# The values of the last two samples in split fp32r matmuls, in a two-layer hybrid decoder step

## The reference

```python
def past_kv(i):
    kp = cache_k[i, page_table].reshape(db, past_len, MOBA_HEADS, HEAD_DIM)
    vp = cache_v[i, page_table].reshape(db, past_len, MOBA_HEADS, HEAD_DIM)
    return kp, vp
...
        logits = jnp.where(allowed, logits, NEG_INF)
        p = jax.nn.softmax(logits.reshape(bsz, h, qc, r * MOBA_BLOCK), axis=-1).reshape(logits.shape)
        return jnp.einsum('bhqrs,bhqrsd->bhqd', p, vg.astype(jnp.float32)).astype(q.dtype)
```

## Time and profile before

| | us |
|---|---|
| median of 3 runs | 1311.08 (1310.75 to 1311.32) |
| span of the profiled execution | 1312.0 |
| TensorE busy | 1158.5 (88%) |
| VectorE busy | 734.8 (56%) |
| ScalarE busy | 570.3 (43%) |
| GpSimd busy | 265.6 (20%) |
| bytes read from HBM | 176.12 MB, 139 GB/s over the span |

### The profile page before, as it was taken

How to read it: one execution, slowest core, us unless ns; L and a number is a source line. 1 busy time by engine, 2 the same in 40 slices (tenths; PEclk the granted TensorE clock), 3 DMA queues, 4 the chain that set the end, 5 groups by cost and what they waited for, 6 DMA issues and landing times.

```text
span 1312.0 us, 21126 instructions
## 1 busy us (share of the span) xinstructions
PE 1158.5 (88%) x7223; PEld 999.5 (76%) x7223; DVE 734.8 (56%) x1165; ACT 570.3 (43%) x959; POOL 265.6 (20%) x250
## 2 busy tenths in 40 slices
PE   6999699787788778888979999997999799999995
PEld 4999588454445444442969999997999699999994
DVE  4843624486767666661366666444565566666333
ACT  3347202344654555541274444334424454444334
POOL 8301015100444445420220000021201220000011
PEclk9989859789989999999989999999999999999997
DMA  7324000433766666645624534433434334543421
GB/s 235 135 89 154 20 1 1 136 137 126 228 194 208 205 216 202 195 156 162 199 65 146 174 128 141 163 121 128 128 130 157 107 128 130 177 140 130 147 83 41
DMA packets 119112, 182.48 MB, mean 139 GB/s; under 512 B 6128, under 2 KB 59471, under 8 KB 118990
## 3 DMA queue, kind: packets, MB, share of 16 engines
q1 hardware_dynamic: 116274, 173.30, 40.5%
q0 software_dynamic: 2784, 8.47, 2.3%
HBM read 176.12 MB, written 5.63 MB: 139 GB/s over the span
## 4 chain that ended last, share of the span: by engine, by line
PE 70%; DVE 12%; ACT 9%; issue 5%; DMA 2%; POOL 1%; SPq 1%; DVEq 0%; ACTq 0%; POOLq 0%
PE bank L1621 65%; DVE kTl L1081 3%; ACT prob L899 2%; ACT kTh L686 2%; PE bank L1905 2%; ACT hi L686 1%; ACT xres L966 1%; POOL xl L629 1%; DVE xres L1081 1%; DMA vring<-cache_v 1%; DVE pen L1407 1%; PE bank L1922 1%; DVE prob L1416 1%; DVE rk L1081 1%; ACT xh L686 1%
## 5 line engine op out<-in xcount | busy, mean ns | idle before, releaser
L1621 PE MATMUL bank<-xh,hi 128*128 128x320 f32 x1184 | 372.9, 315 | 32.4 <-POOL xl L629 26.4
L1621 PE MATMUL bank<-xl,hi 128*128 128x320 f32 x1184 | 370.5, 313 | 0.0
L1621 PE MATMUL bank<-xh,lo 128*128 128x320 f32 x1184 | 370.4, 313 | 0.0
L1074 DVE TENSOR_TENSOR lo<-raw,hi 128x2048 fp32r<-128x2048 f32 x102 | 241.3, 2367 | 196.7 <-ACT hi L686 196.7
L1621 PEld LDWEIGHTS bank<-xh,hi 128*128 128x128 f32 x1184 | 226.7, 192 | 35.2 <-issue 29.8
L686 ACT ACTIVATE hi<-raw 128x2048 fp32r (+1 forms) x102 | 194.7, 1909 | 107.6 <-PE bank L1621 102.5
L1621 PEld LDWEIGHTS bank<-xl,hi 128*128 128x128 f32 x1184 | 226.9, 192 | 0.1
L1621 PEld LDWEIGHTS bank<-xh,lo 128*128 128x128 f32 x1184 | 226.4, 191 | 0.0
L606 POOL TENSOR_TENSOR lo<-vring,hi 128x1024 fp32r<-128x1024 f32 x48 | 114.6, 2390 | 177.6 <-ACT hi L686 177.6
L1081 DVE TENSOR_TENSOR kTl<-bank,kTh 128x512 fp32r<-128x512 f32 x128 | 87.6, 685 | 91.1 <-ACT kTh L686 89.7
L1621 PE MATMUL bank<-hh,hi 128*128 128x320 f32 x416 | 129.5, 311 | 1.3 <-DVE hraw L1081 1.3
(11 more groups left out here) (373 smaller groups left out, 1585.0 us busy)
## 6 DMA issues: line engine op xcount, KB each, us to landing
raw<-w_up SPq DMA_DIRECT2D x44, 1024.0 KB
kring<-cache_k SPq DMA_DIRECT2D x128, 256.0 KB, 3.7
vring<-cache_v SPq DMA_DIRECT2D x128, 256.0 KB, 3.3
raw<-w_down SPq DMA_DIRECT2D x8, 2048.0 KB
raw<-w_in_mix SPq DMA_DIRECT2D x7, 2048.0 KB
raw<-w_in_sc SPq DMA_DIRECT2D x8, 1024.0 KB
raw<-w_down SPq DMA_DIRECT2D x4, 1536.0 KB
raw<-w_out_mix SPq DMA_DIRECT2D x2, 2048.0 KB
```

Of the source, the lines that this page charges most:

```text
L1074: dve.tensor_tensor(lo[:, p], weight(n)[:, :, 256 * p:256 * p + 256], hi[:, p], ALU.subtract)\
L1621: return pe.matmul(out, lhsT, rhs, start=start, stop=stop, **kw)
```

## The change

`WHOLE` becomes `NB`, so that `whole(c)` is false for all samples: samples 6 and 7 take the way of the other six on every engine (rounding of V on ScalarE, difference on GpSimd, difference of the probabilities on VectorE, two fp32r matmuls a page, release of a ring group by `v_lo`). `split_hi(S_OUT, 1)` moves behind ScalarE's wait for `attn_mm`, since the tile half that it writes is in use for the rounded V until then.

```diff
--- before.py
+++ after.py
@@ -335,7 +335,7 @@
         UNITS, VUNITS = 16, 8
 
         pTf = raw[:, PAST + 512:PAST + 512 + 32 * (NPG + 1)].rearrange("p (j r) -> p j r", r=32)
-        WHOLE = NB - 2
+        WHOLE = NB
 
         def whole(c):
             return isinstance(c, int) and c >= WHOLE
@@ -941,9 +941,9 @@
             attend(NB - 2, NB - 3, NB - 4, NB - 1)
             attend(NB - 1, NB - 2, NB - 3, None, 1)
             attend(None, NB - 1, NB - 2)
-            split_hi(S_OUT, 1)
             attend(None, None, NB - 1)
             PE.wait(act, "attn_mm")
+            split_hi(S_OUT, 1)
             AC.up(copy(xh[:, 4:8, SEQ:TOK], bank[6][:, 0:256].rearrange("p (h c) -> p h c", h=H)), "attn_endh")
```

## The result

The changed kernel takes 1333.9 us (median of 4 runs, 1331.4 to 1334.7) against 1311.2 for the kernel before in the same series: ratio 1.0167, 95% interval 1.0152 to 1.0182, so 20 to 24 us slower. A second series in turns, longer and with more runs of before (17), gave 1332.7 against 1312.1: 1.0151, interval 1.0129 to 1.0172, so 17 to 23 us. The forecast was 1327, with a range up to 1333. Runs of one and the same kernel spread by some 8 us over these series (before: 1308.3 to 1316.4), so for terms of 1 to 5 us I read stage lengths within single profiles, which repeat better: the changed kernel profiled twice gave 28.2 and 28.2 for the first of its two stages, 26.9 and 27.2 for the second.

What follows compares the result with a forecast made beforehand. Bound: a round trip over V's ring of two groups, 6.3 us of load plus holding time. Later attn_mm 11.1, exposed splits 3.9 and lower clock 1.0 sum to +16.0 us on the 1311.1 median: 1327, range 1320 to 1333.

Steps and rivals of the forecast that it cites:

- (g): TensorE's clock at the projection and attention's last matmuls: lower level costs 1.0 us, bounds 0 and 3.
- (d): Three round trips of one V ring half, 12.2 us each, 36.6 in sum against 31.5: another 5.1 us.
- (a): Way into sample 6's first groups: sample 7's last bias on VectorE starts at about 582.0, +1.1 us.
- (b): Sample 7's ranks and shifts on VectorE, stretched beside GpSimd's differences: +2.8 us, bounds 0 and 4.6; shifts done 588.6.
- (c): After shifts, exponentials, then unit 3's copy and difference: ring's second half released at 594.2 instead of 588.9, late by 5.3.
- (e): Tail after the last difference: one unit and two own-key halves on TensorE, ending 632.5 against 621.43.
- (f): Splits of S_OUT half 1 between attn_mm and the projection, no longer hidden: gap 4.8 us instead of 0.92, +3.9.
- No price in (b) and (g): Rival: small VectorE operations slip into gaps; only delay (a), round trips and splits remain: +12, 1323; chance 0.20.
- TensorE is the bound: Rival: halves arrive in time in the last stages, TensorE's saving is won: about 8.6 us faster, 1302.5; chance 0.02.
- The stages hide the differences: Rival: GpSimd runs ahead, loads alone limit, (f) and little else remain: +5, 1316; chance 0.05.
- More collisions: Rival: VectorE operations or the clock hold up GpSimd or TensorE, two more 2.3 us waits: +20 to +21, 1332; chance 0.10.
- the opening claim: Values of samples 6 and 7: bound is a V ring round trip, 6.3 us load plus a group's holding time.

Runs made afterwards that it cites:

- e12: Changed kernel without the lo half of V for samples 6 and 7 (no differences, one matmul a page, less exact outputs): -0.1 us over before.
- e8: Changed kernel with V groups 2 and 3 of samples 6 and 7 loaded into the free K ring: +15.8 us over before.
- e4: Changed kernel with split_lo(S_OUT, 0) moved from the tenth stage into idle VectorE time in the first: +16.4 us over before.
- e1: Kernel before with only split_hi(S_OUT, 1) moved behind the wait for attn_mm: +3.3 us over before.
- e5: Changed kernel with four extra unused matmuls behind each unit of values but the last of samples 6 and 7: +16.0 us over before.
- e11: Changed kernel with the rounding of unit 3 of sample 6 ahead of sample 7's exponentials on ScalarE: +18.8 us over before.
- e6: e4 plus sample 7's differences of V made by VectorE instead of GpSimd: +12.0 us over before.
- e7: Kernel before, unsplit fp32, with V groups 2 and 3 of samples 6 and 7 loaded into the free K ring: -7.0 us over before.
- e10: Changed kernel with xh and xl ahead of half 1's splits, split_lo(S_OUT, 0) early, and sample 7's differences on VectorE: +7.0 us over before.
- e3: Kernel before with only sample 6 going through the halves, sample 7 staying in unsplit fp32: +12.6 us over before.

## Why the prediction was wrong

Direction and mechanism were right; the size was 16.0 us against 19.8 by stages. The first median, 1333.9, lies 0.9 us above the range; that of the second series, 1332.7, lies inside it. The step that failed is the price of TensorE's lower clock, (g), and after it the collision that (d) took for hidden. Step by step, in the time of the profile after, which reaches sample 6 0.6 us sooner:

- (a), the bias behind the difference of the probabilities: 582.0 forecast, less 0.6; it started at 581.46. Right.
- (b), ranks beside GpSimd: shifts done at 588.6 less 0.6; measured 587.99. Right, and by the forecast mechanism: 3.08 us for the pair. e12 took the differences away and the pair was back at 0.35. This is also the rule of the Trainium skill ("SBUF — State Buffer", section "SBUF: two separate sides") at work, in both directions: one of GpSimd's differences took 4.2 us beside VectorE's as well.
- (c), the half of the ring released: 594.2 less 0.6; the difference of unit 3 ended at 591.12 + 2.34 = 593.5. Right.
- (d), three round trips: 36.6 forecast, 38.2 measured (593.5 to 631.66). The trips end at 605.2, 619.8 and 631.7: 11.7, 14.6 and 11.9. The middle one holds the collision with `split_lo(S_OUT, 0)`. That the others came near 12.2 is luck in part: the first did not wait for its load but for TensorE, and takes the same 11.7 in e8, where no load is in it. I had written that this split stays hidden and put the collision among the rivals, "in slack". e4 prices it at 1.7. What failed here is "so they fit": the sum of busy times said so, but the two differences of a group stand in series with the load, and 2 us lost in one of them is lost.
- (e), the tail: 1.7 forecast, 3.0 measured (631.66 to 634.7). Same instructions, at the lower clock.
- (f), the splits at the end: 3.9 forecast, 3.7 measured in the changed kernel and in e1. Right.
- (g), the clock: **the term that was mis-sized.** 1.0 taken out of 0 to 3. Measured: 1.3 in (e), 0.8 in the small matmuls (1.87 instead of 1.05), 1.4 in the projection, which starts at the lower clock and stays there for 6.0 us, not 3.2: 3.5 us outside the trips. So the projection was sized nearly right (1.0 against 1.4), and the last unit and the small matmuls at the lower level, named as a bound of up to 2 and then left out of the sum, were 2.1. e5, which kept the clock up with useless work, won 2.9 back ahead of the projection. Both profiles of the changed kernel show the term alike, but kernels close to it pay less of it: e11 has the small matmuls at full clock and the rest of before.

With 1.6 in (d), 1.3 in (e), 0.8 and 0.4 in (g) and -0.2 in (f), the difference between 16.0 and 19.8 is accounted for to 0.1 us. The upper end of the range allowed for this sum (1312.0 + 19.8 would be 1331.8) but not for medians of four runs on top of it.

The rivals. *No price in (b) and (g)* fell with the 3.08 us of the ranks and with e5. *TensorE is the bound* was wrong as the trips show. Its condition, a difference under 1.25 us, is met in e6's tenth stage (1.17), and the stage is 20.7 us there, no shorter than in fp32: the condition was not enough. Of the kernels that round V only e12, without differences, gets both stages below their old length. *The stages hide the differences* fell with e12 too: 19.7 us of the stages go with the differences, the second matmuls and the later release. *More collisions* was in part what happened. And the opening claim, that the bound was a round trip over a ring of two groups, was tested by itself in e7: 7.0 us faster. For the changed kernel it was only half of the truth: e8 took the loads out of the trips and won 2.2 to 2.6 by its stages, since rounding, difference and matmul of a unit through two places of `vh` make a loop of nearly the same length (four units in 10.4 us at the end of e8, 11.9 with the loads), and the ninth stage waits for softmax and differences. That loop was not in my sum.

Open: how the ninth stage's 8 us divide between the exclusion and the exponentials. e11 showed that the order of the two doesn't matter, e12 that the 8 us go with the differences and what hangs on them. Open too: what decides how long the projection runs at the lower clock. Differences on VectorE for sample 6 too, between its softmax operations, were not tried.

## What to carry to other kernels

Replacing a slow matmul by two fast ones is a trade of one engine's time for three other engines' time per byte; at the end of a pipeline, where nothing else hides them, the slowest of the three sets the pace, and every buffer that it reads is held longer. Count an engine's helper instructions twice: for their own length and for what they shut out on the other engine, here VectorE and GpSimd against each other. When a stage turns from busy to waiting, price its matmuls at the lower clock, in the stage and in the one that follows, and keep a microsecond or two of range for it.

## What the runs showed of the hardware

- A difference of 1024 columns with both inputs in SBUF takes 2.34 to 2.45 us on GpSimd alone (before and changed) and 1.17 to 1.23 on VectorE (e6, e10). While one of these runs on one engine, an operation on the other with both inputs in SBUF stands: 3.08 us instead of 0.35 for two rank operations beside two back-to-back differences, 4.20 instead of 2.37 for a difference beside a 2.27 us one of VectorE. The biases and the maxima of VectorE beside GpSimd's differences kept their 0.67 us.
- With less work on TensorE its granted clock was lower: 0.60 and 0.62 where the fp32 matmuls had 1.00, and with 56 useless matmuls (e5) 0.93 and 0.86, with the two stages 2.1 us shorter.
- The lower level lasts into the next stage: 16 plain fp32 instructions took 9.35 us in e3 behind the waiting stage, 7.05 before. Behind one and the same wait of 4.66 us the projection ran at it for 2.8 to 6.2 us (e6, e11, e4, e1, e5, changed, e8).
